# The weight tiles of a two-block model on Trainium2: one DRAM tensor laid out load by load, in place of twelve matrices

## The reference

```python
# first block
mod = silu(c) @ ada_w + ada_b                       # 6 x 2048 values: shifts, scales, gates
h = rmsnorm(x, norm1_g) * (1 + sc1) + sh1
z = h @ w_in                                        # q, k, v of three attention branches, gates, lx, ly, ga, gb
merged = sigmoid(ga) * (attention(z) @ proj_a) + sigmoid(gb) * (recurrence(z) @ proj_b)
x = x + g1 * (merged @ w_out)
h = rmsnorm(x, norm2_g) * (1 + sc2) + sh2
gate, val = split(h @ ffn_up)
x = rmsnorm(x + g2 * ((gelu(conv(gate)) * val) @ ffn_down), final_g)
# second block
q, k, v, a_gate, u, z, g_a, g_s = split(rms_norm(x) @ w_in_2)
y_a = (window_attention(q, k, v) * silu(a_gate)) @ w_attn_proj_2
glu_a, glu_b = split(gelu(state_space(u)) @ w_glu_2 + b_glu_2)
y_s = (glu_a * sigmoid(glu_b) * silu(z)) @ w_ssm_proj_2
x = x + (sigmoid(g_a) * y_a + sigmoid(g_s) * y_s) @ w_out_2
```

## Time and profile before

| | before |
|---|---|
| median of three runs | 2935.36 us |
| lowest and highest | 2929.67, 2937.55 us |
| the profiled execution's own time | 2938.42 us |
| its span, first to last instruction | 2936.7 us |
| mean granted TensorE clock | 0.947 |
| moved by DMA | 564.98 MB, mean 192 GB/s |
| busy: PE, DVE, ACT | 2647.1, 1891.6, 1123.1 us |
| issue to landing, median: `w_in`, `ada_wT`, `ffn_up` | 5.2, 5.3, 5.1 us |

### The profile page before, as it was taken

The page is one execution under the profiler, slowest core; times in us unless marked ns, Lnnn a source line. Parts: engine busy times, 40 slices in busy tenths (PEclk is TensorE's granted clock), DMA queues, the critical chain, the costliest instruction groups (busy, mean ns, idle before and its releaser), DMA issues.

```text
span 2936.7 us, 48131 instructions
## 1 busy us (share of the span) xinstructions
PE 2647.1 (90%) x20558; PEld 2567.0 (87%) x20558; DVE 1891.6 (64%) x2584; ACT 1123.1 (38%) x1379; POOL 197.2 (7%) x166
## 2 busy tenths in 40 slices
PE   2399766799999999989999999999898888889999
PEld 2389766799999999989999999999898777788999
DVE  7864344557676667478975556554468877777663
ACT  1122222356543333334443344434333344433432
POOL 0000000000000000000066540000000000000000
PEclk7698788999999999999999999999999899899999
DMA  8765322345577777457766665554464433345554
GB/s 342 290 255 206 126 77 84 115 137 180 189 280 269 275 278 281 171 200 264 268 208 210 218 226 180 181 186 166 135 204 153 131 125 117 132 146 172 173 201 144
DMA packets 242486, 564.98 MB, mean 192 GB/s; under 512 B 11072, under 2 KB 15168, under 8 KB 229856
## 3 DMA queue, kind: packets, MB, share of 16 engines
q1 hardware_dynamic: 233664, 530.31, 52.3%
q0 software_dynamic: 8608, 31.59, 2.9%
HBM read 549.28 MB, written 12.58 MB: 191 GB/s over the span
## 4 chain that ended last, share of the span: by engine, by line
PE 73%; DVE 14%; DVEq 4%; DMA 4%; ACT 2%; issue 2%; PEldq 0%; PEld 0%; ACTq 0%; POOL 0%; SPq 0%
PE pair L1545 65%; DVE wlo L1102 3%; DVE wraw L1079 2%; DMA wraw<-ada_wT_dram 2%; DMA wraw<-w_in_dram 1%; PE pair L1551 1%; ACT whi L1097 1%; PE bank L401 1%; DVEq L995 1%; PE pair L1538 1%; PE bank L577 1%; DVEq L821 1%; PE bank L337 1%; DVE sx L993 1%; DVE si L1003 1%
## 5 line engine op out<-in xcount | busy, mean ns | idle before, releaser
L1102 DVE TENSOR_TENSOR wlo<-wraw,whi 128x1024 fp32r<-128x1024 f32 x809 | 1000.7, 1251 | 848.0 <-ACT whi L1097 826.2
L1097 ACT ACTIVATE whi<-wraw 128x1024 fp32r<-128x1024 f32 x809 | 844.3, 1057 | 1555.2 <-PE pair L1545 951.2
L1545 PE MATMUL pair<-h_hi,whi 128*128 128x256 f32 x4128 | 1202.8, 291 | 103.2 <-DVE wlo L1102 87.5
L1545 PE MATMUL pair<-h_lo,whi 128*128 128x256 f32 x4128 | 1188.0, 288 | 0.0
L1545 PE MATMUL pair<-h_hi,wlo 128*128 128x256 f32 x4128 | 1186.5, 287 | 0.0
L1545 PEld LDWEIGHTS pair<-h_hi,whi 128*128 128x128 f32 x4128 | 814.7, 197 | 125.8 <-issue 120.2
L1545 PEld LDWEIGHTS pair<-h_lo,whi 128*128 128x128 f32 x4128 | 814.2, 197 | 0.5
L1545 PEld LDWEIGHTS pair<-h_hi,wlo 128*128 128x128 f32 x4128 | 812.7, 197 | 0.0
L1079 DVE SCALAR_TENSOR_TENSOR wraw<-wraw,cb 128x2048 f32<-128x2048 f32 x96 | 218.8, 2288 | 30.7 <-DMA wraw<-ada_wT_dram 29.5
L1545 PE MATMUL pair<-hid_hi,whi 128*128 128x256 f32 x768 | 218.5, 284 | 0.0
L1545 PE MATMUL pair<-hid_lo,whi 128*128 128x256 f32 x768 | 217.3, 283 | 0.0
(11 more groups left out here) (390 smaller groups left out, 3152.3 us busy)
## 6 DMA issues: line engine op xcount, KB each, us to landing
wraw<-w_in_dram SPq DMA_DIRECT2D x172, 1024.0 KB, 5.2
wraw<-ada_wT_dram SPq DMA_DIRECT2D x96, 1024.0 KB, 5.3
wraw<-ffn_up_dram SPq DMA_DIRECT2D x96, 1024.0 KB, 5.1
wraw<-ffn_down_dram SPq DMA_DIRECT2D x48, 1024.0 KB, 5.1
wraw<-w_out_dram SPq DMA_DIRECT2D x32, 1024.0 KB, 5.1
wraw<-proj_a_dram SPq DMA_DIRECT2D x16, 1024.0 KB, 6.8
wraw<-proj_b_dram SPq DMA_DIRECT2D x16, 1024.0 KB, 6.1
turns_scratch<-turned POOLq DMA_DIRECT2D x16, 512.0 KB, 6.1
```

Of the source, the lines that this page charges most:

```text
L1097: sc.activation(whi[:, r, 0:w], wraw[:, z % RAW, 1024 * half:1024 * half + w], ACT.Copy).then_inc(hi_ready, 1)
L1102: ve.tensor_tensor(wlo[:, z % RAW, half, 0:w], wraw[:, z % RAW, 1024 * half:1024 * half + w], whi[:, r, 0:w].bitcast(F32), ALU.subtract).t ...
L1545: ins = te.matmul(pair[:, o, :], w[:, at_w + o * P:at_w + (o + 1) * P], x, start=(k == 0 and o % 2 == 0 and t == 0), stop=(k == last and t ...
```

## The change

The host writes all loads one behind the other into one DRAM tensor `stream` of 501 x 128 x 2048 floats, in the order of `SLOTS`. Tile z holds for partition p exactly the bytes that go to partition p of buffer z % 5. Each load then reads one run of 8 KB a partition (3 KB for the "GATES" slot), and the 128 runs are consecutive. The matrices themselves are no longer inputs. To have the order on the host too, its calculation moves from `build_program` into a function `schedule()`; the list, the ring, the waits and the order of every engine's instructions stay as they are (line numbers shift by some lines: SP's issue is now at L1473 for every load).

```diff
+def schedule():
...
+    return GR, of, U0, U1, SLOTS, HEAD, unit_slot, behind, ada_no
...
-            if slot[0] == "ada":
-                src = W["ada_wT"][slot[1] * P:(slot[1] + 1) * P, :]
-                sp.dma_start(wraw[:, z % RAW, :], src).then_inc(w_loaded[z % RAW], 16)
-                continue
-            gr, s = GR[slot[1]], slot[2]
-            if gr.mode == "GATES":
-                src = W[gr.w][:, gr.col:gr.col + 48].rearrange("(k p) n -> p k n", p=P)
-                dst = wraw[:, z % RAW, 0:DC * 48].rearrange("p (k n) -> p k n", n=48)
-            else:
-                src = W[gr.w][4 * P * s:4 * P * (s + 1), gr.col:gr.col + CB].rearrange("(k p) n -> p k n", p=P)
-                dst = wraw[:, z % RAW, :].rearrange("p (k n) -> p k n", k=4)
-            sp.dma_start(dst, src).then_inc(w_loaded[z % RAW], 16)
+            n = DC * 48 if slot[0] == "w" and GR[slot[1]].mode == "GATES" else 2048
+            sp.dma_start(wraw[:, z % RAW, 0:n], stream[z, :, 0:n]).then_inc(w_loaded[z % RAW], 16)
...
+    GR, slots = schedule()[0], schedule()[4]
+    tiles = np.zeros((len(slots), P, 2048), np.float32)
+    for z, slot in enumerate(slots):
+        if slot[0] == "ada":
+            tiles[z] = v["ada_w"][0][:, slot[1] * P:(slot[1] + 1) * P].T
+            continue
+        gr, part = GR[slot[1]], slot[2]
+        n, k0, k1 = (48, 0, D) if gr.mode == "GATES" else (CB, 4 * P * part, 4 * P * (part + 1))
+        block = W[gr.w][k0:k1, gr.col:gr.col + n].reshape(-1, P, n).transpose(1, 0, 2).reshape(P, -1)
+        tiles[z, :, 0:block.shape[1]] = block
+    stream = dram("stream", tiles)
```

More of the change, by code:

```diff
@@ L99, in groups, with build_program @@
     return out, of
-def build_program(nc, ctx, xT, vecs, cvec, W, small, turns_dram, outT):
+def schedule():
+    GR, of = groups()
+    U0, U1 = [], []
+    at = 0
+    for gr in GR:
+        U0.append(at)
+        at += gr.units
+        U1.append(at)
+    SLOTS, HEAD = [], []
+    unit_slot = {}
+    behind = {}
+    for g, gr in enumerate(GR):
+        for s in range(gr.slots):
+            per = gr.units // gr.slots
+            if g == 0:
+                HEAD.append(range(len(SLOTS), len(SLOTS) + 8))
+                SLOTS += [("ada", col + c) for c in range(4 * s, 4 * s + 4) for col in (16, 0)]
+            for n in range(per):
+                unit_slot[U0[g] + s * per + n] = (len(SLOTS), n)
+            SLOTS.append(("w", g, s, U0[g] + (s + 1) * per))
+            for col in gr.ada.get(s, ()):
+                behind.setdefault(U0[g] + (s + 1) * per - 1, []).append(len(SLOTS))
+                SLOTS.append(("ada", col))
+    N_ADA = 0
+    ada_no = {}
+    for z, slot in enumerate(SLOTS):
+        if slot[0] == "ada":
+            ada_no[z] = N_ADA
+            N_ADA += 1
+    return GR, of, U0, U1, SLOTS, HEAD, unit_slot, behind, ada_no
+def build_program(nc, ctx, xT, vecs, cvec, stream, small, turns_dram, outT):
     base = 16640
@@ L241, in build_program @@
     block = ctx.enter_context(nc.Block())
[L243 to L268, removed]
-        if slot[0] == "ada":
-            ada_no[z] = N_ADA
-            N_ADA += 1
+    GR, of, U0, U1, SLOTS, HEAD, unit_slot, behind, ada_no = schedule()
+    N_UNITS, N_ADA = U1[-1], len(ada_no)
     where = []
@@ L1618 @@
     xT = dram("xT", v["x"][0].T)
-    W = {name: dram(name, v[name][0]) for name in ("w_in", "proj_a", "proj_b", "w_out", "ffn_up", "ffn_down")}
-    W["ada_wT"] = dram("ada_wT", v["ada_w"][0].T)
-    W.update({name: dram(name, v[name]) for name in ("w_in_2", "w_attn_proj_2", "w_glu_2", "w_ssm_proj_2", "w_out_2")})
-    W["ffn_down0"], W["ffn_down1"] = W["ffn_down"][0:FF // 2, :], W["ffn_down"][FF // 2:FF, :]
+    W = {name: v[name][0] for name in ("w_in", "proj_a", "proj_b", "w_out", "ffn_up")}
+    W.update({name: v[name] for name in ("w_in_2", "w_attn_proj_2", "w_glu_2", "w_ssm_proj_2", "w_out_2")})
+    W["ffn_down0"], W["ffn_down1"] = v["ffn_down"][0, 0:FF // 2, :], v["ffn_down"][0, FF // 2:FF, :]
+    GR, slots = schedule()[0], schedule()[4]
+    tiles = np.zeros((len(slots), P, 2048), np.float32)
+    for z, slot in enumerate(slots):
+        if slot[0] == "ada":
+            tiles[z] = v["ada_w"][0][:, slot[1] * P:(slot[1] + 1) * P].T
[5 more added lines that the diff above has]
+    stream = dram("stream", tiles)
     B = np.zeros((8, 4, 2, 16, 2, 2, 64), np.float32)
@@ L1641 @@
     with ExitStack() as ctx:
-        build_program(nc, ctx, xT, vecs, cvec, W, small, turns_dram, outT)
+        build_program(nc, ctx, xT, vecs, cvec, stream, small, turns_dram, outT)
     r = run(nc, [arrays], core_ids=[0])
```

## The result

| | before | changed |
|---|---|---|
| median of 17 runs | 2933.0 us | 2941.86 us |
| lowest and highest | 2927.51, 2937.55 | 2937.95, 2945.45 |
| ratio of the times, 95% interval | | 1.0031 (1.0024 to 1.0039) |
| profiled execution, own time | 2938.42 | 2943.11 |
| its span | 2936.7 | 2941.4 |

The change makes the kernel slower, by 8.9 us between the medians. The two profiles lie only 4.7 us apart, because the profiled execution of before, 2938.42 us, was slower than any of its 17 runs; sizes are therefore taken from the medians and only places from the profiles.

The account below looks back on a forecast made before the run. PE was taken to bound the kernel (90% busy), loads mostly hidden; 0.6 us from lone loads plus 0.5 from the load at 184.91 made 1.1 us less, forecast 2934 us. Own range 2928 to 2939, 8-in-10 range 2922 to 2941.

Parts of the forecast that it names:

- "Slower": Whole kernel: slower by more than 0.3% (8.8 us), chance 0.11, from POOL's packets 0.07 and half the clock case 0.04.
- Packets, bytes, full stretches, issue: SP's queue: 233664 packets become 76608, same 530 MB; PE as full from 800-1240 and 1460-2110 us; issue 368 against 340 ns.
- The lone loads: Eight weight loads alone on the chain, 329.77 to 1334.79 us: 0.08 us less each, 0.6 us in all, bounds 0 and 1.0.
- most of a landing is start and receipt: Lone loads, 4.95 against 4.87 us: packet size does not touch most of such a landing, so only 0.08 us less.
- The load at 184.91: Weight load of 10.26 us beside POOL's second `wcmp` transfer: 0.5 us less, about 9.8 us; bounds nothing and 5.3 us.
- No wait, instruction or transfer is added: Whole span: nothing added and nothing moved to another place of its queue, so no further term in the sum.
- `wcmp` itself lands later by as much, hidden: POOL's second `wcmp` transfer: lands 0.5 us later, hidden because PE first does the units waiting for the load at 184.91.
- The second rival: State-space stage from 2181 us: POOL's `turns` and `bz` wait behind 8 KB packets, 2.3 us a pair, 2945 to 2972 us; chance 0.07.
- The third rival: Attention, 345 to 600 us: earlier landings shift units against clock falls, 10 us either way, 2924 or 2944 us; chance 0.08.
- The first rival: All 122 ACT waits for weight loads count: 10 to 16 us less, 2919 to 2926 us; chance 0.12.

## Why the prediction was wrong, point by point

- **Forecast**: 2934 us, no difference. Measured 2941.86, slower by 0.31%, just over the bound of what can be told apart, and outside the range by 0.9 us. "Slower" had a chance of 0.11.
- **Packets, bytes, full stretches, issue**: right. 76608 packets; SP's issue is now 328 ns at the median.
- **The lone loads**: the sign was right and the term too small. 0.08 us a load was read from three ada loads against eight weight loads; measured are 0.2, because loads in this form are now faster than the ada loads were, and ada loads themselves went from 4.87 to 4.70 us. Why they did, with unchanged packets, no run isolates. In the two kernels whose weights come from the one tensor in 2 KB pieces they have 4.77 and 4.74 us, so the weights' packets are not what did it. Even so the term is under 2 us. That most of a landing is start and receipt was said too strongly: by the prediction's own numbers 2.58 of 4.95 us are the full-queue time.
- **The load at 184.91**: forecast 9.8 us, measured 8.85 and 8.75. Right in kind, as the longer packets gave SP a larger share of the engines.
- **The step that failed** is the sum's claim that "No wait, instruction or transfer is added", with no term for POOL's first set. I looked at the collision that was on the chain, where the weight load was the one that waited. For that one even the half sentence that "`wcmp` itself lands later by as much, hidden" held: the second set's `w` lands at 201.7 us, and PE comes to it at 220.9. But I never looked at its twin 34 us earlier, where POOL's first `wcmp` transfer ran beside the weight loads with 1.1 us in hand. It was not on the chain, so it got no term. There `w` landed 2.9 us later behind its issue, PE waited 2.1 us, and the lower clock behind that cost 8.2 us. The slack of a transfer that is just not on the chain is a number like any other; here it was to be read from two lines, the landing of `w` at 159.1 us and PE's matmul at 160.24.
- **The second rival** had the right mechanism, long packets ahead of POOL's transfers, and the wrong place. At `turns` and `bz` nothing happened: `bz` on the chain went from 3.59 to 3.26 us, `turns` from a median of 3.5 to 3.6. The rule of the Trainium skill (DMA: Bandwidth & Descriptors, SWDGE vs HWDGE vs iDMA), that an engine changes queue only at the end of a packet, agrees with the 130 packets against 130 and 62 against 64 in the two traces above, and with the kernels that have loads 36 to 50 in either size.
- **Its price** was wrong too. I priced a wait for what it lasts, 2.3 us, so that four pairs were needed to get slower. One wait of 2 us was enough, since the lower clock level behind it cost three to four times as much. The third rival spoke of the clock, but only of the attention stage, where it falls anyway, and not of the place where it was 1.00 and could be lost.
- **The first rival** (all 122 waits of ACT count) did not come about: ACT still waits for loads for 538 us in 121 places, 11.5 us less than before, and PE gained nothing in the full stretches.

## What to carry to other kernels

Before transfers are made faster, look for other transfers that share the DMA engines with them, and write down for each when it lands and when it is needed; here the change of packet size moved time from one queue to the other, while it saved a little in all. Price a wait of PE in a stretch of full clock by what the matmuls behind it take at the lower level, not by its length. And where such a wait can't be moved, a few useless matmuls in it may keep the clock, as nine did here.

## What the runs showed of the hardware that was not expected

- PE idle for 1.84 to 3.17 us just before the 64 matmuls was followed in each of five traces by a granted clock of 0.50 and by 11.8 to 13.6 us for them (idle 1.84, 1.87, 2.12, 2.70 and 3.17 us; 11.82, 12.42, 13.59, 12.55 and 13.59 us). Idle for 0.28 to 0.37 us, in three traces, it was followed by 7.33 to 7.36 us at full clock.
- Two queues with work for the same DMA engines share them by packets. The weight load beside POOL's first set took 11.7 to 11.9 us in pieces of 2 KB (three traces) and 8.1 to 8.5 in runs of 8 KB (four); the one beside the second set 10.3 to 11.7 (10.26, 10.48 and 10.37, and 11.29 and 11.73 where all weights are in 2 KB pieces of the one tensor) against 8.7 to 9.1 (8.85, 8.75, 8.71, 9.14); and one beside 4 MB of POOL's 11.79 and 12.31 us against 8.7.
- 1 MB in pieces of 2 KB lands later from consecutive addresses (5.24 to 5.50 us, two traces) than from rows 53 KB apart (4.76 to 5.14 us, three traces); in runs of 8 KB from consecutive addresses 41 of 42 lone weight loads took 4.64 to 4.87 us and one 5.28.
